# Differential attention's norm: a head's squares taken by GpSimd in one piece and summed by VectorE, ScalarE only copies the blocks out

## The reference, cut to what matters

```
def rms_norm(x, g):
    xf = x.astype(jnp.float32)
    ms = jnp.mean(xf * xf, axis=-1, keepdims=True)
    return (xf * lax.rsqrt(ms + LN_EPS) * g.astype(jnp.float32)).astype(x.dtype)

def diff_attention(q, k, v, lam, lam_init, subln_g):
    ...
        p = jax.nn.softmax(logits, axis=-1)
        attn = p[:, :, 0] - lam * p[:, :, 1]
        return jnp.einsum('bhts,bshe->bthe', attn.astype(v.dtype), v)

    o = from_blocks(lax.map(block, (to_blocks(q, Q_BLOCK), jnp.arange(nblk))))
    o = rms_norm(o, subln_g) * (1.0 - lam_init)
    return o.reshape(bn, s, B_WIDTH)
...
    mix = jnp.concatenate([out_a, out_b, out_c], axis=-1)
    x = layer_norm(DEEPNORM_ALPHA * x + jnp.einsum('bse,ed->bsd', mix, w_out), ln1_g, ln1_b)
```

## Time and profile before

| what | us |
|---|---|
| median of 3 executions | 2485.75 |
| lowest and highest of them | 2481.89, 2487.95 |
| the profiled execution, device time | 2484.37 |
| its span in the trace | 2482.2 |
| attention stage in the trace, places 0 to 54, about | 360 to 564 |

### The profile page before, as it was taken

One profiled execution on the slowest core, in us unless ns is written; L12 is line 12 of the kernel. 1 busy time (PEld: TensorE's weight loads), 2 busy tenths in 40 slices (PEclk: granted clock), 3 DMA queues, 4 the chain that ended last, 5 costly groups with the idle time before them and its releaser, 6 DMA issues.

```text
span 2482.2 us, 31284 instructions
## 1 busy us (share of the span) xinstructions
PE 2376.1 (96%) x11999; PEld 1922.5 (77%) x11999; DVE 1495.6 (60%) x2510; ACT 962.7 (39%) x1834; POOL 671.6 (27%) x382
## 2 busy tenths in 40 slices
PE   8999978889999999999999999999899999999998
PEld 6678866777888777777888777777688888888886
DVE  3588998662776777854226578773674555453225
ACT  3467837771222322232212355563533223231212
POOL 3013210000233545542222321110223445442220
PEclk9999988999999999999999999999999999999999
DMA  5026451214314454545332210001421322243333
GB/s 177 9 64 191 153 178 56 98 31 154 122 55 140 149 161 145 168 163 192 102 106 90 71 52 27 28 26 69 144 77 57 96 86 69 85 144 111 102 111 119
DMA packets 219980, 259.21 MB, mean 104 GB/s; under 512 B 16540, under 2 KB 150188, under 8 KB 219832
## 3 DMA queue, kind: packets, MB, share of 16 engines
q1 hardware_dynamic: 219832, 257.22, 31.7%
HBM read 197.36 MB, written 59.82 MB: 104 GB/s over the span
## 4 chain that ended last, share of the span: by engine, by line
PE 79%; DVE 11%; DMA 4%; ACT 3%; issue 1%; POOL 1%; SPq 0%; POOLq 0%; DVEq 0%; ACTq 0%
PE bank L546 10%; PE bank L548 10%; PE bank L547 10%; PE bank L1878 7%; PE bank L1879 7%; PE bank L1880 7%; PE bank L520 6%; PE bank L521 6%; PE bank L522 6%; PE bank L1387 2%; PE bank L2512 1%; DMA early<-in_w_cond 1%; DVE res L1322 1%; PE bank L2481 1%; PE bank L565 1%
## 5 line engine op out<-in xcount | busy, mean ns | idle before, releaser
L498 POOL TENSOR_TENSOR wl<-raw,wh 128x1024 fp32r<-128x1024 f32 x117 | 298.3, 2566 | 1333.0 <-ACT wh L481 1312.9
L546 PE MATMUL bank<-wh,yh 128*128 128x512 f32 x704 | 277.9, 395 | 5.5 <-DVE sum3l L1843 2.8
L547 PE MATMUL bank<-wl,yh 128*128 128x512 f32 x704 | 275.3, 391 | 0.0
L548 PE MATMUL bank<-wh,yl 128*128 128x512 f32 x704 | 275.3, 391 | 0.0
L481 ACT ACTIVATE wh<-raw 128x1024 fp32r<-128x1024 f32 x117 | 123.1, 1060 | 308.5 <-PE bank L548 291.5
L493 POOL TENSOR_TENSOR wl<-res,wh 128x512 fp32r<-128x512 f32 x144 | 197.9, 1397 | 151.0 <-ACT wh L478 130.3
L1878 PE MATMUL bank<-yh,wh 128*128 128x512 f32 x576 | 225.2, 391 | 0.0
L1880 PE MATMUL bank<-yh,wl 128*128 128x512 f32 x576 | 224.2, 389 | 0.0
L1879 PE MATMUL bank<-yl,wh 128*128 128x512 f32 x576 | 224.1, 389 | 0.0
L493 POOL TENSOR_TENSOR wl<-raw,wh 128x512 fp32r<-128x512 f32 x108 | 157.6, 1474 | 228.6 <-ACT wh L478 228.6
L520 PE MATMUL bank<-yh,wh 128*128 128x512 f32 x448 | 180.2, 402 | 8.3 <-DVE yl L583 8.3
(11 more groups left out here) (345 smaller groups left out, 5385.9 us busy)
## 6 DMA issues: line engine op xcount, KB each, us to landing
early<-in_w_cond SPq DMA_DIRECT2D x96, 256.0 KB, 3.0
raw<-in_w_gu SPq DMA_DIRECT2D x44, 512.0 KB, 4.1
raw<-in_w_down SPq DMA_DIRECT2D x44, 512.0 KB, 3.6
raw<-in_w_in SPq DMA_DIRECT2D x40, 512.0 KB, 4.1
qk_d<-res SPq DMA_DIRECT2D x36, 512.0 KB, 4.2
raw<-in_w_gate SPq DMA_DIRECT2D x22, 512.0 KB, 4.2
raw<-in_w_up SPq DMA_DIRECT2D x22, 512.0 KB, 4.2
res<-in_x SPq DMA_DIRECT2D x16, 512.0 KB, 9.8
```

Source lines behind the costliest of these rows:

```text
L498: pool.i.tensor_tensor(wl[n % NU][:, :], raw_of(u)[:, :], wh[n % NU][:, :].bitcast(F32), ALU.subtract).then_inc(*po.up(("wl", u)))
L546: pe.i.matmul(bank[:, 0:wide], xa, h[:, c:c + wide], start=k == 0, stop=False)
L547: pe.i.matmul(bank[:, 0:wide], xa, l[:, c:c + wide], start=False, stop=False)
L548: last = pe.i.matmul(bank[:, 0:wide], xb_, h[:, c:c + wide], start=False, stop=k == nk - 1)
```

## The change

ScalarE's second instruction on each block goes, and its copy now gives the PSUM bank back. GpSimd gets one instruction per head: when the head's eighth block is in `osb`, it writes the squares of all 1024 columns to `tcum` (`pool_subln`). VectorE sums them in groups of 128 with one reduction and goes on as before. Since these two come in between, every step of the norm moves by one place: mean and root from lag 5 to lag 6, the scaling of the blocks and their store from lag 6 to lag 7.

```diff
@@ act_outputs @@
-            act.i.activation(osb[g % 2][:, 128 * i:128 * i + 128], bank[:, 0:128], ACT.Copy, scale=rc).then_inc(*av.up())
-            act.wait_ge(*av.now())
-            act.i.activation(junk_a[:, 0:128], bank[:, 0:128], ACT.Square, scale=rc,
-                             accum_out=small(("subln", g), 24)[:, i:i + 1]).then_inc(*av.frees(uses, tile))
+            act.i.activation(osb[g % 2][:, 128 * i:128 * i + 128], bank[:, 0:128], ACT.Copy, scale=rc).then_inc(*av.frees(uses, tile))
@@ new, and dve_subln @@
+        def pool_subln():
+            for h in range(4):
+                pool.wait_ge(*av.after((place_of["b", h, 7], "out")))
+                for i in (6, 7):
+                    pool.wait_ge(*dv.after(("chosen", i)))
+                pool.wait_ge(*dv.after(("squares", h - 1)))
+                pool.i.tensor_tensor(tcum[:, :], osb[h % 2][:, :], osb[h % 2][:, :], ALU.mult).then_inc(*po.up(("squares", h)))
+
         def dve_subln(h):
             ss = small(("subln", h), 24)
-            dve.wait_ge(*av.after((place_of["b", h, 7], "out")))
+            dve.wait_ge(*po.after(("squares", h)))
+            dve.i.tensor_reduce(ss[:, 0:8], tcum[:, :].rearrange("p (b c) -> p b c", b=8), AX.X, ALU.add).then_inc(*dv.up(("squares", h)))
+            dve.wait_ge(*dv.now())
             dve.i.tensor_scalar(ss[:, 0:8], ss[:, 0:8], 1.0 / 128, LN_EPS, ALU.mult, ALU.add).then_inc(*dv.up(("subln_var", h)))
@@ act_attend, and the same in dve_attend @@
-                h = last_block(t, 5)
+                h = last_block(t, 6)
                 if h is not None:
                     act_subln(h)
@@ dve_attend, and the same in sp_attend @@
-                h = last_block(t, 6)
+                h = last_block(t, 7)
                 if h is not None:
                     dve_subln_end(h)
@@ pool_program @@
             pool_project()
+            pool_subln()
             pool_out1()
```

## The result

The changed kernel took 2488.59 us in the median of 20 runs (2484.29 to 2495.99), the kernel before 2484.90 us in 20 runs beside it (2478.33 to 2487.96). The ratio is 1.0023 with a 95% interval of 1.0015 to 1.0031: slower by 5.7 us by that ratio (3.7 to 7.7), or 0.23%. The plain difference of the two medians is 3.7 us. The forecast was +6.15 us and, with a chance of 0.66, no difference of more than 0.3%. So the number was right, and in part by luck: of its terms two were too small by several microseconds, with opposite signs.

What follows compares the result with a forecast made beforehand. No engine alone bounds the attention stage: its chain passes between TensorE, VectorE and ScalarE, and its end waits for head 3's norm. -2.0 + 1.7 + 5.65 + 0.8 = +6.15 us, 2491.9 against the median; range 2484.5 to 2498.

Steps and rivals of the forecast that it cites:

- Step 4: Tail of the attention stage: head 3's norm one place later delays the first `ms` load and what follows, +5.65 us.
- Step 5: TensorE behind the `ms` gap: half clock slows the first eight transposes, +0.8 us, bounded by 0 and about 2.
- Step 1: Attention stage: squares leaving ScalarE give only what VectorE's next waits let through, -2.0 us, at most 5.5 us.
- Rival 1: Attention stage: all 12 squares on the chain come off in full, 5.5 us, leaving +1 us overall; chance 0.18.
- Step 2: Attention stage: VectorE's added reduction and moved norm steps of VectorE and ScalarE cost +1.7 us, 1.4 of it at head 1.
- Step 3: GpSimd in the attention stage: one squares operation per head, at most 2.57 us, is hidden and costs nothing.
- rival 2: Attention stage, heads 0 and 2: GpSimd's squares hold VectorE's operations, up to 1.9 us each; +8 to +14 overall, chance 0.20.
- Rivals 3 and 4: Tail delay is covered, -0.3 to -5.5 us, chance 0.06; ScalarE isn't shortened by the change, +8 us, chance 0.06.
- The signs of being wrong: First `ms` transposes under 4 us later behind event 46's weighing, or event 46 ending over 3 us from 558.9.

Runs made afterwards that it cites:

- head3_late: The kernel before, ScalarE's squares kept, with only head 3's norm one place later: ratio 1.0032 against the kernel before, +8.0 us.
- filled: The changed kernel with 32 unused transposes put into TensorE's gap before the first `ms` transposes: ratio 1.0013 against the kernel before.
- no_squares: The kernel before without any squares, the mean taken from the gain vector: ratio 0.9974 against the kernel before, -6.5 us.
- reduction_alone: The kernel before with one more VectorE reduction of `tcum` per head, its result unread: ratio 0.9993 against the kernel before.
- head3_early: The changed kernel with head 3's norm alone back at its old places, heads 0 to 2 late: ratio 0.9997 against the kernel before.
- old_places: The changed kernel with all the norm's steps back at their old lags, GpSimd's squares and the reduction kept: ratio 0.9992 against the kernel before.
- reduction_no_squares: The kernel before without squares but with VectorE's reduction per head, norm at its old places: ratio 0.9977 against the kernel before, -5.7 us.

## Why the prediction was right, and where it wasn't

**Step 4, head 3's norm one place later: right, and it carries the result.** VectorE's inverse should come 5.65 us later, measured against the events. It started 6.99 us ahead of event 46's weighing (548.66 and 555.65), now 1.35 us ahead of it in both profiles (551.71 and 553.06, 548.71 and 550.06): 5.64 us later. That the two agree to 0.01 us is chance: the second profile of before has 7.37 us there (550.36 and 557.73), which would make it 6.0. The root was no hindrance: ScalarE's was done at 550.89. The gap of TensorE should be 5.9 us and is 4.5, because the stores were quicker in the later place. From the scaling's start to the issue of the first `ms` load it is 6.73 us in the profile of before (549.08 and 555.81) and 6.3 to 6.9 us in every other one with head 3 at its old place, but 5.3 us in every one with it late (552.15 and 557.50 in the changed kernel). I had called the work the same and so its duration too. What the stores meet in the old place isn't settled. head3_late confirms the rest: the gap needs no other part of the change.

**Step 5, the clock behind the gap: right in kind, too small by some 4 us.** I gave half clock to the first 8 transposes only, 0.8 us, and bounded it at 2. From start to start, the transposes took 0.84 us more, event 47's weighing 3.20 us more, and what follows up to the products 0.70 us more: 4.7 us. I had followed the clock to the end of one run of instructions, where the trace of before already had a stretch of 5 us at 0.50 behind a wait of TensorE. The step failed in the length that I gave the slow stretch; filled measures it without the wait: 3.9 us.

**Step 1, the squares leave ScalarE: too small by 4.5 us.** -2.0 us stood in the sum, -5.5 us as the most, and no_squares measured -6.5 us. I had let each square give only what the next wait of VectorE would let through, and this is what failed; which of the squares gave more no run tells apart. Rival 1, the squares in full, had this step right; it didn't set the time because steps 2 and 3 took back 4.5 us of the 6.5 and the tail cost more than it said.

**Step 2, reduction and moved steps: the duration right, the price rather too high.** L1428 takes 1.20 us, the value taken from L1098's 1220 ns. The Trainium skill, VectorE: DVE Perf Modes, in "The perf-mode tier table", allows `tensor_reduce` only the slowest mode; the trace agrees, with 1.20 us and not the 0.6 us of my lower end. But four of them cost at most 0.75 us in reduction_alone, not 1.4 us for head 1 alone; with the squares gone the ratios give 0.8 us and can't exclude more. For the moved steps of heads 0 to 2, head3_early beside old_places shows no price that is clear of noise.

**Step 3 and rival 2, GpSimd.** The squares take 1.89 us and not 2.57, and nobody waits for them at the later places. The mechanism of rival 2 is there in one place: of the 32 L1344 one, at head 2, took 1.57 us instead of 0.22 and ended with GpSimd's square (502.54 + 1.89 = 504.43). The Trainium skill, GPSIMD Engine Reference, "Key points", says that operations of VectorE with two inputs from SBUF are in conflict with GpSimd; the trace agrees even for a single column, by that one row. It is 1.35 us at one head and not the rival's 1.9 at two, and not its +8: with the old places the kernel isn't slower at all. But my step 3 put GpSimd at nothing, and no run settles its price: this row has 1.35 us, and the ratios would have 3.7.

**Rivals 3 and 4.** The tail isn't covered; 9.4 us longer says so. The copy on ScalarE stays at 347 ns, and ScalarE is shorter by 15 us.

**The signs of being wrong.** The gap in front of the first `ms` transposes grew by 4.2 us (0.29 to 4.51), just past the 4 us that I had asked for. Event 46 ended 2.6 us ahead of 558.9 in the first profile of the changed kernel (556.30), inside the 3 us, but 5.6 us ahead in the second (553.30). By that one I would have called the forecast wrong; since the unchanged kernel's second profile is itself 2 us off (560.97), the sign was no test.

So the sum was -2.0 + 1.7 + 5.65 + 0.8. By the runs it reads: squares off ScalarE -6.5, reduction and GpSimd together +4.5 (with it old_places, -2.0), later places of heads 0 to 2 about 0, head 3's place +8.0 (head3_late, 5.0 to 10.7; in the traces +9, of which the gap is 4.2). That is +6.0, each term with an uncertainty of some 3 us. The forecast of +6.15 stands so close to +5.7 measured by luck in two places: squares, reduction and GpSimd were -0.3 in my sum and -2.0 in the runs, though the gain alone was three times what I gave it, and head 3's place was 6.45 and is 8.0, with the gap 1.4 us shorter and the clock behind it 4 us dearer than I said.

## What to carry to other kernels

Before an engine is relieved by giving its work a later place, look for the one instance of it that the next stage waits for: three heads could move at no price that the runs can tell, and the fourth cost 8 to 9 us. Price a gap of TensorE as the gap plus the half-speed stretch behind it, and try whether other work, even work without a use, in the gap gives part of it back. Compare two kernels between points that both have, not by the ends of single profiles, and take a second profile of each before a term of a few microseconds is read from one.

## What the runs showed of the hardware that was not expected

- A GpSimd product of one 128x1024 tile with itself takes 1.89 us; the two-input L498 of the same width, which reads two tiles and writes another format, takes 2.57 us in the mean and 2.41 in the median. In pieces of 128 columns the square is 0.40 us for most of them.
- A VectorE operation on one column ended with GpSimd's running operation, 1.56 to 1.57 us instead of 0.22, in each of the six profiles with one square a head. VectorE's L1322, which reads PSUM, took 0.55 us for 384 columns beside a square (401.49 to 403.38) as elsewhere.
- Behind a gap of 4.4 to 4.5 us TensorE ran at half clock for some 10 us (0.50 from 561 to 571), although it had work all that time; with the same gap filled by transposes it ran at full clock. A wait of 1.78 us was followed by a clock of 0.52 for 3.5 us (reduction_no_squares), waits of 0.3 to 0.98 us by full clock.
- Head 3's stores and the wait for them took 5.3 us one place later and 6.3 to 6.9 us at the old place, with the same eight stores.
